# Splitting the experts' down product into three fp32r passes in a decoder-block kernel

## The reference, cut to what matters

```python
def expert_block(args):
    xb, e = args
    gate, up = jnp.split(xb @ w_gate_up[e], 2, axis=-1)
    return (jax.nn.silu(gate) * up) @ w_down[e]
...
y = jnp.zeros((N, D), h.dtype).at[tok_sorted].add(y_disp[dest] * w_sorted[:, None].astype(h.dtype))
```

## Time and profile before

| | us |
|---|---|
| median of 3 runs | 3340.65 (3335.42 to 3342.27) |
| the profiled execution, its own time | 3336.84 |
| its span, first to last instruction | 3334.9 |
| expert stage, first to last down product | about 2605 to 3237 |
| PE busy over the span | 2816.0 (84%) |
| DVE busy | 1495.1 (45%) |
| ACT busy | 1236.6 (37%) |
| mean granted clock of PE | 0.916 of 2.4 GHz |

### The profile page before, as it was taken

How to read it: one execution, slowest core, us unless ns; L and a number is a source line. 1 busy time by engine, 2 the same in 40 slices (tenths; PEclk the granted TensorE clock), 3 DMA queues, 4 the chain that set the end, 5 groups by cost and what they waited for, 6 DMA issues and landing times. The chain is left out here.

```text
span 3334.9 us, 37607 instructions
## 1 busy us (share of the span) xinstructions
PE 2816.0 (84%) x12196; PEld 2030.6 (61%) x12197; DVE 1495.1 (45%) x1910; ACT 1236.6 (37%) x2059; POOL 648.3 (19%) x632
## 2 busy tenths in 40 slices
PE   6999889998859888997799976999660999999980
PEld 5888668886326666665699964444330677677650
DVE  4221042212445555662544424233343677767657
ACT  3123231233416656565211113111220556556543
POOL 0000000000015544443422200000004222222225
PEclk9999989999969989898899988999875999999995
DMA  3122221222331112102544435412370799999969
GB/s 105 44 76 101 95 87 58 71 92 76 125 105 33 34 34 55 34 9 70 164 127 114 138 120 211 173 55 90 119 277 17 283 389 390 391 395 393 384 263 373
DMA packets 161962, 514.43 MB, mean 154 GB/s; under 512 B 36672, under 2 KB 65600, under 8 KB 135776
## 3 DMA queue, kind: packets, MB, share of 16 engines
q1 hardware_dynamic: 137824, 446.40, 38.0%
q0 software_dynamic: 14848, 33.60, 2.7%
q10 hardware_dynamic: 9216, 33.56, 2.5%
HBM read 406.00 MB, written 124.13 MB: 159 GB/s over the span
## 5 line engine op out<-in xcount | busy, mean ns | idle before, releaser
L1882 DVE TENSOR_TENSOR ex_gl<-ba_raw,ex_gh 128x2048 fp32r<-128x2048 f32 x128 | 288.4, 2289 | 217.9 <-ACT ex_gh L1808 217.9
L1808 ACT CAST ex_gh<-ba_raw 128x2048 fp32r<-128x2048 f32 x128 | 238.6, 1903 | 136.8 <-PEq L1431 75.1
L946 POOL TENSOR_TENSOR at_pl<-at_pf,at_ph 128x512 fp32r<-128x512 f32 (+1 forms) x160 | 188.0, 1177 | 314.9 <-ACT at_ph L850 314.9
L847 ACT ACTIVATE at_pf<-at_psS 128x512 f32<-128x512 f32 (+1 forms) x320 | 172.5, 539 | 182.3 <-PE at_psS L756 130.3
L1772 PE MATMUL ex_psY<-ba_raw,ex_hT 128*128 128x512 f32 x512 | 231.1, 594 | 3.7 <-issue 2.3
L879 DVE TENSOR_REDUCE at_nm<-at_psA 128x1 f32<-128x512 f32 (+2 forms) x320 | 184.0, 607 | 106.3 <-PE at_psA L791 63.1
L1751 PE MATMUL ex_psG<-ex_gh,ex_xh 128*128 128x512 f32 x512 | 223.5, 436 | 2.8 <-DVE ex_xl L1887 2.8
L909 DVE TENSOR_TENSOR at_pl<-at_pf,at_ph 128x512 fp32r<-128x512 f32 (+2 forms) x160 | 148.3, 937 | 155.0 <-ACT at_ph L850 153.5
L1753 PE MATMUL ex_psG<-ex_gh,ex_xl 128*128 128x512 f32 x512 | 200.4, 391 | 0.0
L1752 PE MATMUL ex_psG<-ex_gl,ex_xh 128*128 128x512 f32 x512 | 200.0, 391 | 0.0
L922 POOL CAST at_vh<-all_cst 128x32 fp32r<-128x32 f32 x2 | 0.5, 228 | 941.8 <-POOLq L443 941.8
(11 more groups left out here) (317 smaller groups left out, 5940.1 us busy)
## 6 DMA issues: line engine op xcount, KB each, us to landing
ba_raw<-in_w_exp SPq DMA_DIRECT2D x192, 1024.0 KB, 20.6
y_d<-ex_y ACTq DMA_DIRECT2D x64, 512.0 KB
pi_raw<-in_w_slabs SPq DMA_DIRECT2D x32, 512.0 KB, 3.8
pj_raw<-in_w_slabs SPq DMA_DIRECT2D x32, 512.0 KB, 4.0
mx_gt<-gates_d SPq DMA_DIRECT2D x64, 256.0 KB, 5.2
n_xr<-x_d SPq DMA_DIRECT2D x32, 512.0 KB, 5.7
y_d<-xa_zero SPq DMA_DIRECT2D x32, 512.0 KB, 4.8
n_xr<-in_x SPq DMA_DIRECT2D x16, 512.0 KB, 4.6
```

Source lines behind the costliest of these rows:

```text
L847: nc.scalar.activation(pf[:, u % RING, off:CH], psS[u % RING][:, off:CH], ACT.Exp)
L946: G_.tensor_tensor(pl[:, r, off:CH], pf[:, r, off:CH], ph[:, r, off:CH], ALU.subtract).then_inc(lo[0], 1)
L1808: nc.scalar.copy(gh[:, s, i], raw[:, r, i, :].rearrange("p (k n) -> p k n", k=KD // 2)).then_inc(w_hi, 1)
L1882: V.tensor_tensor(gl[:, s, i], raw[:, r, i, :].rearrange("p (k n) -> p k n", k=KD // 2), gh[:, s, i], ALU.subtract).then_inc(w_lo, 1)
```

## The change

The down product is split like gate/up: its weights into `dh` and `dl` (one buffer each), the transposed hidden rows into `hh` and `hl` (two buffers each), and go_down issues 12 fp32r matmuls in place of 4 float32 calls. The raw down weights lie in two slots of their own, `rawd`, in place of four; four experts' gate/up slots stay. ACT copies both halves of the result; DVE's copy is gone. ACT's order in a step becomes `weights_high(b+1)`, `take_h(b-1)`, `sigmoid(b)`, `take_x(b+1)`, `take_y(b-1)`, `down_high(b)`; DVE's becomes `weights_low(b+1)`, `take_h(b-1)`, `hidden(b)`, `take_x(b+1)`, `down_low(b)`. SP asks for the down weights of `e+2` when `down_low(e)` is done. The core of the diff:

```diff
+        dh = s_.sb("dh", [P, 2 * D], F32R)
+        dl = s_.sb("dl", [P, 2 * D], F32R)
...
-        hT = s_.sb("hT", [P, 2, 2, P])
+        hh = s_.sb("hh", [P, 2, 2, P], F32R)
+        hl = s_.sb("hl", [P, 2, 2, P], F32R)
...
+            def next_down(e, s):
+
+                sp.wait_ge(d_lo, e + 1)
+                down_weights(e + 2, s)
+
+            next_halves(0, 0)
+            for r in range(1, RAW):
+                next_halves(r, r)
+                next_down(r - 1, (r - 1) % 2)
...
-                pe.wait_ge(hcopy, b + 1)
+                pe.wait_ge(h_lo, b + 1)
...
-            def go_down(b, s, r, nw):
-                pe.wait_ge(r_in[r][2], nw)
-                pe.wait_ge(hcopy, b + 2)
+            def go_down(b, s):
+                pe.wait_ge(d_lo, b + 1)
+                pe.wait_ge(h_lo, b + 2)
...
-                        mm = nc.tensor.matmul(psY[f][:], hT[:, s, k, :], raw[:, r, 2, k * D + f * CH:k * D + (f + 1) * CH], start=(k == 0), stop=(k == 1))
+                        n = slice(k * D + f * CH, k * D + (f + 1) * CH)
+                        nc.tensor.matmul(psY[f][:], hh[:, s, k, :], dh[:, n], start=(k == 0), stop=False)
+                        nc.tensor.matmul(psY[f][:], hl[:, s, k, :], dh[:, n], start=False, stop=False)
+                        mm = nc.tensor.matmul(psY[f][:], hh[:, s, k, :], dl[:, n], start=False, stop=(k == 1))
...
+            def down_high(b, s, nw):
+
+                act.wait_ge(down, b)
+                act.wait_ge(d_in[s], nw)
+                nc.scalar.copy(dh[:], rawd[:, s, :]).then_inc(d_hi, 1)
+
...
                 nc.scalar.copy(y[:, s, 0:CH], psY[0][:]).then_inc(ya, 1)
+                nc.scalar.copy(y[:, s, CH:], psY[1][:]).then_inc(yv, 1)
...
+                take_h(b - 1, 1 - s)
                 sigmoid(b, s)
-                take_h(b - 1, 1 - s)
                 if more:
                     take_x(b + 1, 1 - s)
                 take_y(b - 1, 1 - s, 16 * (RAW // 2) * t + 16 * ((j - 1) // 2))
+                down_high(b, s, 16 * (RAW // 2) * t + 16 * (j // 2 + 1))
...
+            def down_low(b, s):
+                dve.wait_ge(d_hi, b + 1)
+                V.tensor_tensor(dl[:], rawd[:, s, :], dh[:], ALU.subtract).then_inc(d_lo, 1)
+
+            def take_h(b, s):
+                dve.wait_ge(hcopy, b + 1)
+                V.tensor_tensor(hl[:, s], psH[:], hh[:, s], ALU.subtract).then_inc(h_lo, 1)
...
                     weights_low(b + 1, 1 - s, (j + 1) % RAW)
+                take_h(b - 1, 1 - s)
                 hidden(b, s)
                 if more:
                     take_x(b + 1, 1 - s)
-                take_y(b - 1, 1 - s, 16 * (RAW // 2) * t + 16 * ((j - 1) // 2))
+                down_low(b, s)
...
-            raw = b_.sb("raw", [P, RAW, 3, 2 * D])
+            raw = b_.sb("raw", [P, RAW, 2, 2 * D])
+            rawd = b_.sb("rawd", [P, 2, 2 * D])
```

More of the change, by code:

```diff
@@ L1628, in _, with experts @@
                     nc.gpsimd.indirect_dma_start(tab_d, bass.IndirectOffsetOnAxis(ap=tp[:, a, i:i + 1].bitcast(U32), axis=0), tok[:, i:i + 1], None).then_inc(scat, 16)
-def experts(nc, cst, h_d, w_exp, y_d, tab, meta, raw, r_in):
+def experts(nc, cst, h_d, w_exp, y_d, tab, meta, raw, r_in, rawd, d_in):
     with ExitStack() as ctx:
@@ L1654, in experts @@
             "ixd", "turned", "x_hi", "x_lo", "w_hi", "w_lo", "used", "up", "sig", "gt", "hid", "hturn", "hcopy", "down", "ya", "yv"))
+        h_lo, d_hi, d_lo = s_.sem("h_lo"), s_.sem("d_hi"), s_.sem("d_lo")
         ident = cst[:, C_ID:C_ID + P]
@@ L1681, in load, with down_weights, next_halves @@
                 sp.dma_start(raw[:, r, i, :], w_exp[bass.ds(e, 1), i].rearrange("a p n -> p (a n)")).then_inc(r_in[r][i], 16)
-            with sp.Fori(0, E // RAW - 1) as t:
-                for r in range(RAW):
[L1685 to L1692, removed]
+            def down_weights(e, s):
+                sp.dma_start(rawd[:, s, :], w_exp[bass.ds(e, 1), 2].rearrange("a p n -> p (a n)")).then_inc(d_in[s], 16)
+            def next_halves(e, r):
+                for i in range(2):
+                    sp.wait_ge(w_lo, 2 * e + (i + 1))
+                    load(e + RAW, r, i)
+            def next_down(e, s):
[5 more added lines that the diff above has]
+                next_down(r - 1, (r - 1) % 2)
+            with sp.Fori(1, E // RAW - 1) as t:
+                for r in range(RAW):
+                    next_halves(RAW * t + r, r)
+                    next_down(RAW * t + (r - 1), (r - 1) % 2)
+            for e in range(E - RAW - 1, E - 2):
+                next_down(e, e % 2)
             def more(b):
                 e = sp.value_load(meta[0:1, bass.ds(b - E, 1)], min_val=0, max_val=E - 1)
-                sp.wait_ge(down, b)
-                for i in range(3):
+                sp.wait_ge(d_lo, b)
+                for i in range(2):
                     load(e, 0, i)
+                down_weights(e, 0)
             overflow(sp, more)
@@ L1785, in step @@
                     turn(b + 1, 1 - s, 16 * (RAW // 2) * t + 16 * ((j + 1) // 2 + 1))
-                go_down(b - 1, 1 - s, (j - 1) % RAW, landed(t, j - 1))
+                go_down(b - 1, 1 - s)
             steps(pe, step)
             turn_hidden(E - 1, 1)
-            go_down(E - 1, 1, RAW - 1, 16 * (E // RAW))
+            go_down(E - 1, 1)
             def more(b):
@@ L1795, in more @@
                 turn_hidden(b, 0)
-                go_down(b, 0, 0, 16 * (b - E) + 16 * (E // RAW + 1))
+                go_down(b, 0)
             overflow(pe, more)
@@ L1823, in take_h @@
                 act.wait_ge(hturn, b + 1)
-                nc.scalar.copy(hT[:, s], psH[:]).then_inc(hcopy, 1)
+                nc.scalar.copy(hh[:, s], psH[:]).then_inc(hcopy, 1)
             def take_y(b, s, n):
@@ L1834, in take_y @@
                 act.dma_start(y_d[bass.ts(b, P), :], y[:, s, :]).then_inc(st[s], 16)
-            act.sem_inc(hcopy, 1)
             act.sem_inc(ya, 1)
+            act.sem_inc(yv, 1)
             for s in range(2):
@@ L1844, in _ @@
             take_x(1, 1, True)
+            act.wait_ge(d_in[0], 16)
+            nc.scalar.copy(dh[:], rawd[:, 0, :]).then_inc(d_hi, 1)
             def step(b, t, j, more):
@@ L1864, in more @@
                 take_x(b, 0)
+                down_high(b, 0, 16 * (b - E) + 16 * (E // 2 + 1))
                 sigmoid(b, 0)
@@ L1893, in hidden @@
                 V.tensor_tensor(hm[:, s, :], psG[s][:, FF:], sg[:, s, :], ALU.mult).then_inc(hid, 1)
[L1895 to L1898, removed]
             dve.sem_inc(hid, 1)
-            dve.sem_inc(yv, 1)
+            dve.sem_inc(h_lo, 1)
             weights_low(0, 0, 0)
@@ L1906, in _ @@
             take_x(1, 1)
+            down_low(0, 0)
             def step(b, t, j, more):
@@ L1914, in step @@
                     take_x(b + 1, 1 - s)
-                take_y(b - 1, 1 - s, 16 * (RAW // 2) * t + 16 * ((j - 1) // 2))
+                down_low(b, s)
             steps(dve, step)
-            take_y(E - 1, 1, 16 * (E // 2 - 1))
+            take_h(E - 1, 1)
             def more(b):
@@ L1922, in more @@
                 take_x(b, 0)
+                down_low(b, 0)
                 hidden(b, 0)
-                take_y(b, 0, 16 * (b - E) + 16 * (E // 2))
+                take_h(b, 0)
             overflow(dve, more)
@@ L2119, in program @@
             meta = b_.sb("meta", [1, 40], I32)
-            raw = b_.sb("raw", [P, RAW, 3, 2 * D])
-            r_in = [[b_.sem(f"r_in{r}_{i}") for i in range(3)] for r in range(RAW)]
+            raw = b_.sb("raw", [P, RAW, 2, 2 * D])
+            rawd = b_.sb("rawd", [P, 2, 2 * D])
+            r_in = [[b_.sem(f"r_in{r}_{i}") for i in range(2)] for r in range(RAW)]
+            d_in = [b_.sem("d_in0"), b_.sem("d_in1")]
             def load_first_experts(sp):
                 for e in range(RAW):
-                    for i in range(3):
+                    for i in range(2):
                         sp.dma_start(raw[:, e, i, :], a["w_exp"][e, i]).then_inc(r_in[e][i], 16)
+                    if e < 2:
+                        sp.dma_start(rawd[:, e, :], a["w_exp"][e, 2]).then_inc(d_in[e], 16)
             with nc.sbuf_tensor("hT3", [P, KD, T], F32) as hT:
@@ L2130, in program @@
                 route(nc, cst, hT, a["w_r"], a["b_r"], tab_d, wts, dest, tab, meta, load_first_experts)
-            experts(nc, cst, h_d, a["w_exp"], y_d, tab, meta, raw, r_in)
+            experts(nc, cst, h_d, a["w_exp"], y_d, tab, meta, raw, r_in, rawd, d_in)
             combine(nc, x3_d, y_d, wts, dest, a["g_final"], out)
```

## The result

The changed kernel takes 3702.49 us (median of 4 runs, 3699.83 to 3705.3) against 3340.59 before: a ratio of 1.1086, with a 95% interval of 1.1067 to 1.1106. The forecast was 3720, in a range of 3640 to 3770. The profiled execution took 3705.3 us, 368.5 more than the one before.

What follows compares the result with a forecast made beforehand. PE and the DMA engines were taken to be full at once. To the profiled 3336.8 us came 247 for waits and ends at full clock and 132 for half clock: 3716, or 3720 as median, range 3640 to 3770.

Steps and rivals of the forecast that it cites:

- The ring: Expert stage: waits through ACT, DVE and PE between down products make a full-clock step 13.95 us, against 10.06.
- The clock: Down product: after PE's 4.7 us idle piece it runs partly at half clock, 2.1 us a step, 132 in all.
- the upper bound: Down product: the most that half clock can add, 2.4 us a step, with all 12 matmuls slowed.
- the two longer rows: Attention windows: after 6.20 and 6.00 us idle, PE works at 0.50 for 5.20 and 4.70 us.
- The sum: Whole kernel: 3336.8 us profiled, + 247 + 132 = 3716; the runs' median 3.8 higher, so 3720, 11% slower.
- The hidden gain: Expert stage: loads stand right behind PE, so its saving of 0.78 us a step can't all show.
- The slots: Down weights' loads: two slots for four, some 23 us of cover against 20.4 to land, costed at nothing.
- the smaller lead: Ahead of the expert stage: 2 MB less of weights asked for, costing 5 us.
- the second rival: Expert stage: the loop doesn't close, loads keep the step at 10.06 us, 3346 us in all; chance 0.04.
- The copies of y: ACT, after the down product: two halves of the result copied, 2 x 0.59 = 1.17 us a step.

Runs made afterwards that it cites:

- the kernel with PE kept at work: Changed kernel plus five unused float32 products of constants on PE ahead of each down product: 3583.17 us, 1.0731 of the kernel before.
- the kernel with `hl` between the halves: Changed kernel with DVE's low part of the hidden rows moved between the two gate/up low halves: 3441.84 us, 1.0307 of the kernel before.
- reordered kernel: Changed kernel with all its work, in other orders on ACT and DVE within a step: 3348.87 us, 1.0026 of the kernel before.
- half of the down weights' load: Only the left half of the down weights' columns loaded from the third expert on: reordered kernel 3333.95 us, the kernel with the slots alone 3339.51 us.
- the kernel with the slots alone: Kernel before, float32 down product kept, with only two separate down-weight slots freed by that product: 3338.11 us, 0.9997 of the kernel before.

## Why the prediction was right

**The ring.** Its terms, forecast and then measured in the step shown above: down product to ACT 2.93 at full clock, measured as 3.12 in the kernel with PE kept at work (3000.80 to 3003.92) and 5.26 at half clock (3005.39 to 3010.65); the halves of y 1.17 and 1.07, for the second copy starts 0.48 after the first; store and waits 0.69 and 0.69; `down_high` 1.90 and 1.90, to DVE 0.04 and 0.04; DVE's three subtractions 6.70 and 6.61 (3014.35 to 3020.96); `hl` and PE 0.52 and 0.52. The forecast of the ring at full clock was 13.95 us; the kernel with PE kept at work has 13.85.

**The clock.** Forecast 2.1 us a step, measured 1.98 by that same experiment (15.83 - 13.85). That the clock falls in every such step was right; the size was in part luck. Against 13.85 us, 40 steps lose 2.4 us, which was the upper bound, and 20 lose 1.5; nothing in the earlier trace rows told of this mix, and no step loses 2.1. The half-clock stretch covers 10 or 11 of the 12 down matmuls in the step shown, as the two longer rows had it. In the 61 steps in which PE stood idle for 4.0 to 4.5 us ahead of the down product, the clock fell. Ahead of the first and the 63rd product PE was idle for 1.85 and 0.97 us, and it stayed at 1.00, as it did in the kernel with `hl` between the halves up to its 63rd product (0.1 to 1.44 us idle). The rule of the Trainium skill on the returning wait (TensorE: Matmul & The Clock Gate, "HAM oscillation — how this bites in real kernels") held here in each of those 61 steps.

**The sum.** Ring 3583.17 - 3340.59 = 243 us (forecast 247), clock 3702.49 - 3583.17 = 119 (forecast 132). The forecast was 18 us too high, most of it the clock's.

**The hidden gain.** The prediction began with it: the loads stand right behind PE. The reordered kernel shows it: 9.8 us a step while the weights last, 10.05 over the stage, and 9.83 to the end with less to load. The saving was over-sized, though. By sums PE needs 9.26 us a step; the best order tried runs at 9.8, so that 0.2 us of PE's 0.78 came through even where no load was in the way. One part of the rest is a short wait that the sum of PE's work left out. A step of the reordered kernel with half of the down weights' load:

```profile
3001.53 0.38 PE L1780 MATMUL ex_psH<-all_cst,ex_hm 128*128 128x128 f32 x2
...
3002.35 0.42 DVE L1929 TENSOR_TENSOR ex_hl<-ex_psH,ex_hh 128x256 fp32r<-128x256 f32 x1 [0.81 <-ACT ex_hh L1852]
...
3002.88 0.47 PE L1792 MATMUL ex_psY<-ex_dh,ex_hh 128*128 128x512 f32 x1
```

From the transposes of the hidden rows to the down product it takes 1.35 us, where it took 1.09 before: ACT's `hh` and DVE's `hl` now follow each other there, and `hl` is done only at 3002.77, when PE's ten transposes (1.09 us) are over. That is 0.26 of the 0.57 us between 9.26 and 9.83; the others were not taken apart.

**The slots.** Costed at nothing, and nothing was measured. The 5 us for the smaller lead, in the second rival, were not there either.

**The copies of y.** In the ring as forecast; undone, they give back 25 us of 362.

## What to carry to other kernels

When an operand of a product becomes a split one, write down the ring from one use of its buffer to the next through every engine's program order, and add its pieces up; sums of busy time for each engine (here 9.3, 9.1 and 8.5 us in a step of 10.06) say nothing about it. If the ring is longer than the step, look for the short operation that stands behind long ones it doesn't need: moving one 0.42 us subtraction past one 2.3 us subtraction gave back 261 us of 362. Then look at how long TensorE stands idle in one piece: here the lower clock behind it cost half as much again as the wait itself (119 us on 243).

## What the runs showed of the hardware

- Useless matmuls made the kernel faster: 5 float32 products a step, 4.46 us of PE's time in the idle piece, took 119 us off.
- The DMA engines' busy share does not fall in proportion to the bytes. Windows up to 3050 us of the kernel with the slots alone, then of the same with half of the down weights' load:

```profile
2605.00:3050.00 445.00, 445.00 (x1876) 315.69 (x1875) 317.37 (x310) 269.16 (x312) 110.97 (x132) 1.00 0.99 390
```

```profile
2605.00:3050.00 445.00, 445.00 (x1870) 315.04 (x1869) 315.35 (x310) 268.00 (x311) 110.90 (x132) 1.00 0.94 339
```

  The rate falls by 13%, as the bytes do, the share by 5%. A share near 1 beside a full PE doesn't yet say how much faster the loads could go.
- ACT starts a copy before the record of its last one is over: the second half of y begins 0.48 us after the first, which lasts 0.59. The forecast counted 0.59 twice.
- In the step shown, PE's first down matmul behind the wait, at half clock, costs 3005.95 - 3005.39 = 0.56 us, the others 0.43.
